# Keys-by-queries scores in the prompt attention of a hybrid encoder, with a maxima pass and inverses spread as rows

## What is computed

```python
def _dense_attention(q, k, v, qpos, kpos, frame_causal, fq=None, fk=None):
    scale = q.shape[-1] ** -0.5
    kc = kpos // CHUNK
    def block(qb, qpb, *fqb):
        s = jnp.einsum('bqhd,bkhd->bhqk', qb, k, preferred_element_type=jnp.float32) * scale
        if fk is not None:
            s = s + jnp.swapaxes(fqb[0], 1, 2)[..., :, None] - jnp.swapaxes(fk, 1, 2)[..., None, :]
        qp = qpb[0]
        if frame_causal:
            allowed = kpos[None, :] <= qp[:, None]
        else:
            allowed = kc[None, :] <= (qp // CHUNK)[:, None]
        s = jnp.where(allowed, s, NEG_INF)
        p = jax.nn.softmax(s, axis=-1)
        return jnp.einsum('bhqk,bkhd->bqhd', p.astype(v.dtype), v)
```

## Time and profile before

| | |
|---|---|
| median of 3 runs | 3323.08 us (3322.79 to 3323.21) |
| the profiled execution | 3319.49 us |
| its span, first to last instruction | 3317.7 us |
| mean granted TensorE clock | 0.935 of 2.4 GHz |
| FoX prompt attention, layer 0 and 1 | 125.7 and 127.6 us |
| MLA prompt attention, layer 0 and 1 | 88.3 and 87.4 us |

### The profile page before, as it was taken

One profiled execution on the slowest core, in us unless ns is written; L12 is line 12 of the kernel. 1 busy time (PEld: TensorE's weight loads), 2 busy tenths in 40 slices (PEclk: granted clock), 3 DMA queues, 4 the chain that ended last, 5 costly groups with the idle time before them and its releaser, 6 DMA issues. The chain is left out here.

```text
span 3317.7 us, 50480 instructions
## 1 busy us (share of the span) xinstructions
PE 2993.8 (90%) x19996; PEld 2799.5 (84%) x19996; DVE 1575.9 (47%) x2735; ACT 992.2 (30%) x2175; POOL 860.9 (26%) x488
## 2 busy tenths in 40 slices
PE   7998877677999999999999998867679999999998
PEld 6997755456999999999899975636479999999998
DVE  3336655734344444444441474657333444444443
ACT  4224535534311111111232253445433111111111
POOL 3112141113422232223331123311143232222230
PEclk9998968788999999999999997788889999999999
DMA  5110100002511111111131101000034111111111
GB/s 182 37 42 22 40 11 18 1 9 63 169 58 38 51 50 38 40 49 43 51 102 47 41 2 40 10 17 1 13 98 149 51 38 51 38 51 38 51 51 53
DMA packets 181248, 161.79 MB, mean 49 GB/s; under 512 B 17236, under 2 KB 168316, under 8 KB 180860
## 3 DMA queue, kind: packets, MB, share of 16 engines
q1 hardware_dynamic: 181116, 160.02, 15.6%
HBM read 129.97 MB, written 30.13 MB: 48 GB/s over the span
## 5 line engine op out<-in xcount | busy, mean ns | idle before, releaser
L1954 PE MATMUL bank_b<-x_hi,fwhi 128*128 128x352 f32 x2112 | 690.1, 327 | 5.3 <-POOL fwlo L1910 5.3
L1954 PE MATMUL bank_b<-x_hi,fwlo 128*128 128x352 f32 x2112 | 688.4, 326 | 0.0
L1954 PE MATMUL bank_b<-x_lo,fwhi 128*128 128x352 f32 x2112 | 686.7, 325 | 0.0
L1910 POOL TENSOR_TENSOR fwlo<-raw,fwhi 128x1024 fp32r<-128x1024 f32 x132 | 321.9, 2439 | 583.3 <-ACT fwhi L2035 569.2
L1954 PEld LDWEIGHTS bank_b<-x_hi,fwhi 128*128 128x128 f32 x2112 | 399.4, 189 | 6.5 <-POOL fwlo L1910 5.9
L1954 PEld LDWEIGHTS bank_b<-x_lo,fwhi 128*128 128x128 f32 x2112 | 401.7, 190 | 0.0
L1954 PEld LDWEIGHTS bank_b<-x_hi,fwlo 128*128 128x128 f32 x2112 | 398.4, 189 | 0.6
L2143 DVE TENSOR_TENSOR fx<-fx,bank_b 128x352 f32<-128x352 f32 x528 | 275.3, 521 | 233.5 <-PE bank_b L1984 233.5
L1984 PE MATMUL bank_b<-fuhi,fwhi 128*128 128x352 f32 x1056 | 344.1, 326 | 10.2 <-DVE fx L2143 5.7
L1984 PE MATMUL bank_b<-fulo,fwhi 128*128 128x352 f32 x1056 | 344.5, 326 | 0.0
L1984 PE MATMUL bank_b<-fuhi,fwlo 128*128 128x352 f32 x1056 | 344.0, 326 | 0.0
(11 more groups left out here) (410 smaller groups left out, 5965.8 us busy)
## 6 DMA issues: line engine op xcount, KB each, us to landing
raw<-in_w_ffn_up SPq DMA_DIRECT2D x88, 512.0 KB, 3.9
raw<-in_w_ffn_down SPq DMA_DIRECT2D x44, 512.0 KB, 3.6
wraw<-in_w_in SPq DMA_DIRECT2D x18, 984.0 KB, 5.4
xs<-x_between SPq DMA_DIRECT2D x16, 528.0 KB, 4.1
x_between<-xs SPq DMA_DIRECT2D x16, 528.0 KB, 2.6
fx<-x_between SPq DMA_DIRECT2D x2, 4224.0 KB, 13.3
raw<-in_w_out SPq DMA_DIRECT2D x16, 512.0 KB, 5.3
x_between<-fx SPq DMA_DIRECT2D x3, 1408.0 KB, 6.3
```

The lines of the kernel that those rows point to most:

```text
L1910: pool.tensor_tensor(self.wlo[:, r], self.raw[:, o % 2], self.whi[:, r].bitcast(F32), ALU.subtract)\
L1954: last = pe.matmul(bank[:, first_bank + t, 0:TN], w[:, role, c, :], x[:, c, self.cols(t)], start=(c == 0 and m == 0), stop=(c == DC - 1 an ...
```

## The change

A new function `attend_keys` takes the place of `attend_prompt` for FoX and MLA. It computes the scores as keys x queries, so that exp writes what the V product reads and no probability is transposed. Since the maximum of a query then lies across partitions, a first pass (high x high only, queries x keys) gives the maxima: DVE reduces it (with the mask where the block is on the diagonal, `tensor_tensor_reduce`), PE turns the maxima to a row, and that row stands as one more row of q against a row of ones in k. The forget bias takes two rows (high and low). Work goes in units u of one head pair and 512 queries (4 or 8 blocks of keys); the next unit's first pass and the next tiles are hosted in the steps of the current one. The sums of exp are added block by block (POOL for one head, DVE for the other), summed over keys by matmuls with one column of ones (`denominators`), inverted a query per partition, and spread as rows by matmuls with the identity (`inverses`); DVE multiplies yT with them.

```diff
@@ scalar_first
-        act.activation(k.mfoxr[:, :], k.const[:, C_MFOX:C_MFOX + P], ACT.Copy)
-        act.activation(k.mmlar[:, :], k.const[:, C_MMLA:C_MMLA + P], ACT.Copy)
+        one = k.const[:, C_ONE:C_ONE + P]
+        act.activation(k.mfoxr[:, :], k.const[:, C_TRI:C_TRI + P], ACT.Copy, scale=-BIG, bias=BIG)
+        act.activation(k.mmlar[0:CHUNK, :], one[0:CHUNK], ACT.Copy, scale=0.0)
+        act.activation(k.mmlar[CHUNK:P, 0:CHUNK], one[CHUNK:P, 0:CHUNK], ACT.Copy, scale=BIG)
+        act.activation(k.mmlar[CHUNK:P, CHUNK:P], one[CHUNK:P, CHUNK:P], ACT.Copy, scale=0.0)
@@ new function
+def attend_keys(nc, k, kind, heads, kdim, x_tile, v_of, yT, yc, mask, maskr, frow=None):
...
+    R0, NA = kdim, 3 if fox else 1
+    K1, K2 = kdim + NA - 1, kdim + NA
+    XS = 2
+    NP = 3
+    nb = lambda u: HT * (u % 2 + 1)
+    first_col = lambda u, b: max(b - HT * (u % 2), 0) * P
...
+    def max_units(u):
+        if u % 2 == 0:
+            return [(e, j, 0, (j + 1) * P, True) for j in range(HT) for e in range(2)]
+        return [(e, j, a, w, a > 0) for j in range(HT) for a, w in ((0, HALF), (HALF, (j + 1) * P)) for e in range(2)]
+    def hosted_tiles(u, b):
+        p = u // 2
+        if u % 2 == 0:
+            return [(p, HT + 2 * b), (p, HT + 2 * b + 1)] if b < 2 else []
+        return [(p + 1, b)] if b < HT and p + 1 < pairs else []
+    def hosted_units(u, b):
+        if u + 1 == NU:
+            return []
+        units = max_units(u + 1)
+        if u % 2 == 0:
+            at = (0, 4, 10, 16, 16)
+        else:
+            at = (0, 0, 0, 0, 2, 4, 6, 8, 8)
+        return units[at[b]:at[b + 1]]
...
+        def bank_free(pe, item):
+            n = bank_of[item] - 2
+            if n < 0:
+                return
+            what = order[n]
+            if what[0] == "aux":
+                pe.wait_ge(aux_hi, 2 * what[1] + what[2] + 1)
+                pe.wait_ge(aux_lo, 2 * what[1] + what[2] + 1)
+            elif what[0] == "s":
+                pe.wait_ge(expd, 2 * step_no[what[1:3]] + what[3] + 1)
+            elif what[0] == "den":
+                pe.wait_ge(inverted, what[1] + 1)
+            else:
+                pe.wait_ge(y_done, what[1] + 1)
...
+        def sum_up(eng, u, b, e, done):
+            n, c = step_no[(u, b)], first_col(u, b)
+            new = pT[:, n % NP, e, c:HALF]
+            eng.wait_ge(expd, 2 * n + e + 1)
+            if b == 1:
+                old = pT[:, (n - 1) % NP, e, :]
+                if u:
+                    eng.wait_ge(den_done, u)
+                if c:
+                    eng.tensor_copy(acc[:, e, 0:c], old[:, 0:c])
+                eng.tensor_tensor(acc[:, e, c:HALF], old[:, c:HALF], new, ALU.add).then_inc(done, 1)
+            else:
+                eng.wait_ge(done, sums_to(u, b) - 1)
+                eng.tensor_tensor(acc[:, e, c:HALF], acc[:, e, c:HALF], new, ALU.add).then_inc(done, 1)
...
+            def _(pool):
+                for n, (rows, value) in enumerate(((kh[R0:K2].bitcast(F32), 1.0), (mtab[:, 0:HALF - P], 0.0),
+                                                   (kl[R0:K2].bitcast(F32), 0.0))):
+                    pool.memset(rows, value).then_inc(cleared, 1)
+                    pool.wait_ge(cleared, n + 1)
+                pool.tensor_copy(mtab[:, HALF - P:HALF], mask).then_inc(cleared, 1)
+                for u, b in steps:
+                    if b == 0:
+                        continue
+                    sum_up(pool, u, b, 0, sum0)
...
+                def first_pass(u, units):
+                    p, s = divmod(u, 2)
+                    for e, j, a, w, _ in units:
+                        n = unit[0]
+                        pe.wait_ge(x_hi, tile_no(p, HT * s + j) + 1)
+                        if n >= 2:
+                            pe.wait_ge(maxed, n - 1)
+                        if fox:
+                            pe.wait_ge(row_in[p % 2], 64 * (p // 2 + 1))
+                        pe.matmul(psS[:, n % 2, 0:w], qh[0:K1, s, e, j * P:(j + 1) * P], kh[0:K1, p % 2, e, a:a + w],
+                                  start=True, stop=True).then_inc(scored, 1)
+                        unit[0] += 1
+                def maxima(u):
+                    pe.wait_ge(maxed, unit_base[u + 1])
+                    for e in range(2):
+                        item = ("aux", u, e)
+                        bank_free(pe, item)
+                        for j in range(HT):
+                            last = pe.transpose(psT[0:NA, bank_of[item] % 2, j * P:(j + 1) * P], mc[:, u % 2, j, e, :],
+                                                ident)
+                        last.then_inc(aux_done, 1)
+                def scores(u, b):
+                    p, s = divmod(u, 2)
+                    c, diag = first_col(u, b), b >= HT * s
+                    if b == 0:
+                        pe.wait_ge(aux_lo, 2 * u + 2)
+                        pe.wait_ge(x_lo, tile_no(p, HT * s + HT - 1) + 1)
+                    for e in range(2):
+                        item = ("s", u, b, e)
+                        bank_free(pe, item)
+                        out = psT[:, bank_of[item] % 2, :]
+                        keys = slice(b * P, (b + 1) * P)
+                        pe.matmul(out[:, c:HALF], kh[0:K2, p % 2, e, keys], qh[0:K2, s, e, c:HALF], start=True, stop=False)
+                        pe.matmul(out[:, c:HALF], kl[0:K2, p % 2, e, keys], qh[0:K2, s, e, c:HALF], start=False, stop=False)
+                        last = pe.matmul(out[:, c:HALF], kh[0:K2, p % 2, e, keys], ql[0:K2, s, e, c:HALF], start=False,
+                                         stop=not diag)
+                        if diag:
+                            last = pe.matmul(out[:, c:c + P], k.identr[:, :], maskr, start=False, stop=True)
+                        last.then_inc(s_done, 1)
+                def values(u, b):
+                    p, n, c = u // 2, step_no[(u, b)], first_col(u, b)
+                    pe.wait_ge(expd, 2 * n + 2)
+                    if b == 0 and u:
+                        pe.wait_ge(y_copied, u)
+                    for e in range(2):
+                        last = pe.matmul(psO[HD * e:HD * e + HD, c:HALF], v_of(2 * p + e, b), pT[:, n % NP, e, c:HALF],
+                                         start=(b == 0), stop=(b == nb(u) - 1), skip_group_check=True)
+                    last.then_inc(mixed, 1)
+                def denominators(u):
+                    item = ("den", u)
+                    bank_free(pe, item)
+                    for e, done in enumerate((sum0, sum1)):
+                        pe.wait_ge(done, sums_before(u + 1))
+                        for j in range(HT):
+                            at = e * HT + j
+                            last = pe.matmul(psT[:, bank_of[item] % 2, at:at + 1], acc[:, e, j * P:(j + 1) * P],
+                                             ones[:, 0:1], start=True, stop=True)
+                    last.then_inc(den_done, 1)
+                def inverses(u):
+                    item = ("inv", u)
+                    bank_free(pe, item)
+                    pe.wait_ge(inverted, u + 1)
+                    for j in range(HT):
+                        for e in range(2):
+                            last = pe.matmul(psT[HD * e:HD * e + HD, bank_of[item] % 2, j * P:(j + 1) * P],
+                                             rec[:, e, j:j + 1].broadcast_to([P, HD]), ident, start=True, stop=True)
+                    last.then_inc(inv_done, 1)
...
+                first_pass(0, max_units(0))
+                maxima(0)
+                for u, b in steps:
+                    for p, i in hosted_tiles(u, b):
+                        turn(p, i)
+                    if b == 1 and u:
+                        inverses(u - 1)
+                    scores(u, b)
+                    if b == 0 and u:
+                        denominators(u - 1)
+                    first_pass(u + 1, hosted_units(u, b))
+                    if b:
+                        values(u, b - 1)
+                    if b == nb(u) - 1:
+                        if u + 1 < NU:
+                            maxima(u + 1)
+                        values(u, b)
+                denominators(NU - 1)
+                inverses(NU - 1)
...
+                for u, b in steps:
+                    for p, i in hosted_tiles(u, b):
+                        high_part(p, i)
+                    n, c = step_no[(u, b)], first_col(u, b)
+                    if n >= NP:
+                        act.wait_ge(mixed, n - NP + 1)
+                        act.wait_ge(sum0, sums_to(*steps[n - NP]))
+                        act.wait_ge(sum1, sums_to(*steps[n - NP]))
+                    for e in range(2):
+                        act.wait_ge(s_done, 2 * n + e + 1)
+                        act.activation(pT[:, n % NP, e, c:HALF], psT[:, bank_of[("s", u, b, e)] % 2, c:HALF], ACT.Exp)\
+                           .then_inc(expd, 1)
+                    if b == nb(u) - 1:
```

(51 more changed lines are left out.)

123 lines of the change are left out of this document (added).

## The result

The changed kernel takes 3598.8 us (median of 4 runs, 3591.7 to 3607.1), against 3323.1 for the one before on the same chip: ratio 1.083, 95% interval 1.0807 to 1.0853. The forecast was 3440, with a range of 3383 to 3500. The sign is right, the size is not: the rise is 276 us where 117 were worked out. The profiled execution took 3607.1 us with a span of 3605.2, against 3319.5 and 3317.7.

What follows compares the result with a forecast made beforehand. PE was taken as the bound, with 40.3 (FoX) and 42.1 us (MLA) of work a pair against 38.0; with waits, stages added 70 (FoX) and 48 us (MLA), 118 together: 3440 us, range 3383 to 3500.

Steps and rivals of the forecast that it cites:

- Rival D: Faster: longer runs of one kind shed PE's overhead, 31 to 33 us a FoX pair, 3290 us; chance 0.04.
- Rival E: No change that can be told: FoX pairs of 36.4 us, 3323 us; chance 0.03.
- Rival B: PE alone sets the pace, other waits hidden, 0.8 us idle at each turnover: 3383 us; chance 0.11.
- A: The main case, the summed work and waits: odd (long) unit 26.6 us, whole kernel 3440 us; chance 0.70.
- The sum: Stage by stage total: FoX 161.5 us and MLA 112 us a stage, +118 us for both layers.
- 3437.5: Forecast profiled execution in us: 3319.5 before plus 118; the median was put 3.6 higher.
- the walk through the queues: PE, ACT and DVE followed through an even and an odd unit: 22.9 and 26.6 us, 49.5 a pair.
- the one drop that it had read: Earlier trace, 694.5 to 697.9 us: PE, waiting, was busy 1.43 us and then granted 0.51, 1.2 GHz.
- C: Slower: idle PE drops even units' maxima stretches to 1.2 GHz, 3470 us, or V products serialize; chance 0.12 together.
- The other half of C: Long V products of the two heads run one behind the other: 7.9 us more in ten pairs, 3519 us.
- the 2.4 us set aside for half clock: In a stage's first unit, 2.4 us added for half clock, so its last scores start at 32 us.
- PE waits for DVE's division: Second head's scores need the bank of the inverses, so they wait for the division, in even and odd units.

Runs made afterwards that it cites:

- run 6: The changed kernel with score passes on 128 rows, denominators over 64 columns and filler matmuls that nobody reads: 3496.4 us, ratio 1.0523.
- run 1: The changed kernel with FoX's three score passes on 96 rows instead of 67, the added rows adding nothing: 3566.6 us, ratio 1.0734.
- run 2: The changed kernel with all three score passes on 128 rows in FoX and MLA, padded with zeros: 3528.5 us, ratio 1.0620.
- run 3: The kernel before with fewer score rows: FoX on 65 instead of 96, 3330.1 us; all prompt scores on 32, 3425.4 us.
- run 5: The changed kernel with filler matmuls on 128 rows behind short units' maxima matmuls and ahead of units' first scores: 3549.9 us, ratio 1.0689.

## Why the prediction was right or wrong

**The sign** is right for the reason given: PE is the bound and has more to do, and no wait that went away could pay for it. Rival D, by which longer runs of one kind shed enough of PE's overhead, is refuted by the long unit at full clock: PE is busy 25.4 of 27.1 us, where D needed a whole pair in 36.4. Rival E goes with it. Rival B, waits hidden: the long unit would take PE's own 24 us and 0.8; it takes 27.1. A's 26.6 was nearer.

**The step that failed is the clock.** The sum took 2.4 GHz everywhere but in the first 15 us of a stage. The profiled execution came out 169.6 us above 3437.5, and 161.5 of these lie in the four stages. By part: FoX's five units behind the first of each layer 101 us (179.2 and 168.3 measured, 123.2 forecast), MLA's three 22 us, the first units 29, the ends 9.

That the 101 are the clock is shown by run 6. At full clock a long FoX unit takes 27.2 us (26.6 forecast) and the last 23.1 (24.2). A short one takes 26.4 with 18 filler matmuls inside, and since the two records of one move the next maxima matmul by 0.14 us or more, some 2.5 to 3 us of it are filler (an estimate): 23.4 to 23.9, against 22.9. Two long, two short and the last long are then about 125 us, against 123.2. The MLA units of the changed kernel that were granted 1.00 took 26.7 (27 forecast). For these units the walk through the queues was right within 5%, and its clock was wrong by a factor of up to two. Run 6 as a whole is still 56 us above 3440: in its profiled execution the first units are 27 us above the forecast, the others 21 (filler, and layer 1's short units at 0.88), the ends 5.

**Why the clock step failed.** The prediction asked only where PE would wait, because the one drop that it had read, stood behind a stretch with PE idle. It priced that case for the short units alone: C, 3 us in each of ten, 3470, with a chance of 0.12 for C's cases together. The short units do run at 0.56 to 0.67, and there C's case came out in kind: PE idles 3 to 4 us in them, and they are 8 to 12 us too long rather than 3. But C's 30 us are less than a fifth of the gap. In FoX long units in which PE hardly waits run at 0.54 to 0.83, and two signs that stood in the trace of before and the diff were not weighed: that the scores go from 96 rows to 67, and that the 128-row transposes between them disappear. Runs 1 to 3 show that the rows count by themselves, in either kernel and where they add nothing to the result; run 5 shows that full-height matmuls added to a stretch raise its clock. That the lost transposes did the opposite is argued. The other half of C, V products of two heads one behind the other, is refuted: 1.00 us for four 512-column records (410.81 to 411.81 above), the 1.0 that had been worked out from the earlier trace rows.

**Start of a stage.** The first real scores came 16.8 us behind the first transpose (15.4 forecast): GpSimd's two clearings took 3.5 us each, as worked out from the earlier trace rows. But in FoX the clock stays at 1.2 GHz for all 44.9 us to the first copy-out, where about 35.3 had been worked out, so the 2.4 us set aside for half clock were 9.6 short. **End of a stage**: 4.1 us from copy-out at full clock (3.0 forecast), 6.6 at 1.2 GHz.

**Waits.** PE waits for DVE's division ahead of the second head's scores, as foretold: 1.6 us in two places from 315 to 502 us. At full clock it is more, 1.0 us in a long unit and 2.4 in a short one of run 6; at 1.2 GHz PE arrives late enough to hide it. So at a slow clock the waits look small.

**A size off without effect:** the high and low parts of 128 columns, taken at 0.19 to 0.2 us each, are 0.285 on ACT and 0.297 on DVE from start to start where they change between partitions 0 and 64, as long as they last. Both engines have room for it.

**What stays open.** How much of FoX's loss is the rows and how much the lost transposes or the matmuls that were added; and how these add up, since 65 rows in the kernel before cost only 7 us. For MLA, whose rows did not fall, only the second part is left. The stage of layer 0 has one long unit at 43.2 us where its like in layer 1 takes 30.3, with the same instructions; why the clock fell there and not here is not shown. This kernel's four runs spread over 15 us, with the profiled one the slowest; those of before spread over 1.3 us beside them and over nearly 9 in a series of 11. That such units make the spread was not tried.

## What to carry to other kernels

When an edit lowers the rows of the array that the matmuls use (shown here), or takes full-height transposes out from between them (argued), count its PE time at 1.2 GHz as well as at 2.4 and forecast both, even where PE never waits. Look at the granted clock beside the busy share before anything else: a PE that is 99% busy with fewer instructions than before is slow, not loaded. Where the clock is the loss, extend operands with rows that add nothing, which costs no PE instruction but here 3 to 4 us of clearings at a stage's start, or put full-height work in the gaps. Neither made this change pay (3496.4 with both, against 3323); in a kernel that is at 2.4 GHz already the filler brings 0.15% at the stage starts.

## What the runs showed of the hardware

The rows that single-pass matmuls use count for the granted clock, and not only by groups of 32: 67 and 96 rows both take three groups of 32, and differ by 32 us a kernel (run 1). Rows that hold zeros on both sides count: rows 65 to 95 do in the kernel before, and without them it takes 7 us more (run 3).

A DVE add and a GpSimd add that read distinct parts of SBUF at the same time run one behind the other. Timelines of GpSimd and DVE in the kernel of run 2:

```profile
332.46 1.28 POOL L1059 TENSOR_TENSOR accfox<-accfox,pTfox 128x512 f32<-128x512 f32 x1 [3.18 <-ACT pTfox L1234]
...
332.91 1.38 DVE L1056 TENSOR_TENSOR accfox<-pTfox 128x512 f32<-128x512 f32 x1
...
341.68 0.69 DVE L1059 TENSOR_TENSOR accfox<-accfox,pTfox 128x512 f32<-128x512 f32 x1
```

DVE's add started at 332.91, inside GpSimd's (to 333.74), and ended at 334.29, 0.55 behind it; alone the same shape takes 0.69. The Trainium skill, SBUF — State Buffer, "SBUF: two separate sides", has the rule: a DVE operation with two SBUF inputs and a GpSimd one that reads SBUF lock each other out for a whole instruction. The rows agree. Here it is hidden; in a kernel bound by DVE it would cost up to 0.7 us each time (an estimate, 1.38 less 0.69).
